# Half-width level products and selects in the recurrent stage of a two-block transformer kernel

## What is computed

```
b = jnp.cumsum(lf, axis=2)
o_inter = jnp.einsum('bhtk,bhkv->bhtv', q * jnp.exp(b), state)
diff = b[:, :, :, None, :] - b[:, :, None, :, :]
decay = jnp.exp(jnp.where(causal[:, :, None], diff, NEG_BIG))
scores = jnp.einsum('bhtk,bhsk,bhtsk->bhts', q, k, decay)
o_intra = jnp.einsum('bhts,bhsv->bhtv', scores, v)
```

## Time and profile before

| | |
|---|---|
| median of 3 runs | 1531.72 us |
| lowest and highest run | 1528.85 and 1534.35 us |
| span of the profiled execution | 1527.0 us |
| PE busy | 1477.4 us, 97% of the span, 7613 instructions |
| DVE busy | 811.7 us, 53% |
| ACT busy | 573.6 us, 38% |
| POOL busy | 317.6 us, 21% |
| the stage of this case | from 1043.2 to 1096.8 us of the span |
| TensorE clock, mean of the span | 0.996 of full speed |

### The profile page before, as it was taken

How to read it: one execution, slowest core, us unless ns; L and a number is a source line. 1 busy time by engine, 2 the same in 40 slices (tenths; PEclk the granted TensorE clock), 3 DMA queues, 4 the chain that set the end, 5 groups by cost and what they waited for, 6 DMA issues and landing times. The chain is left out here.

```text
span 1527.0 us, 18721 instructions
## 1 busy us (share of the span) xinstructions
PE 1477.4 (97%) x7613; PEld 1203.3 (79%) x7613; DVE 811.7 (53%) x1122; ACT 573.6 (38%) x905; POOL 317.6 (21%) x304
## 2 busy tenths in 40 slices
PE   7999999999999999999999999999899999999998
PEld 5888787886788888888887776676778888888886
DVE  4232434578656537433355699878846434333425
ACT  4231534457635413223144532385434323112312
POOL 1000100000023897000002289634421000000000
PEclk9999999999999999999999999999999999999999
DMA  4231222220032323232332222110013323232322
GB/s 186 84 110 61 81 67 94 77 84 1 29 128 79 111 83 111 83 110 83 110 110 66 92 75 84 62 56 29 29 56 111 110 83 111 83 110 83 110 70 82
DMA packets 38858, 129.25 MB, mean 85 GB/s; under 512 B 4676, under 2 KB 23004, under 8 KB 27380
## 3 DMA queue, kind: packets, MB, share of 16 engines
q1 hardware_dynamic: 38484, 127.93, 24.4%
q10 hardware_dynamic: 288, 0.12, 0.0%
HBM read 124.82 MB, written 3.17 MB: 84 GB/s over the span
## 5 line engine op out<-in xcount | busy, mean ns | idle before, releaser
L266 PE MATMUL bank<-xT_hi,ring_hi 128*128 128x512 f32 (+2 forms) x928 | 355.2, 383 | 7.2 <-DVE xT_lo L1728 4.8
L266 PE MATMUL bank<-xT_hi,ring_lo 128*128 128x512 f32 (+2 forms) x928 | 351.7, 379 | 0.0
L266 PE MATMUL bank<-xT_lo,ring_hi 128*128 128x512 f32 (+2 forms) x928 | 351.6, 379 | 0.0
L247 DVE TENSOR_TENSOR ring_lo<-ring_raw,ring_hi 128x2048 fp32r<-128x2048 f32 (+3 forms) x112 | 260.2, 2325 | 168.8 <-ACT ring_hi L233 168.6
L233 ACT CAST ring_hi<-ring_raw 128x2048 fp32r<-128x2048 f32 (+4 forms) x114 | 211.0, 1852 | 240.6 <-DMA ring_raw<-in_w_ff 130.6
L266 PEld LDWEIGHTS bank<-xT_hi,ring_hi 128*128 128x128 f32 (+1 forms) x928 | 174.1, 188 | 47.9 <-issue 7.8
L266 PEld LDWEIGHTS bank<-xT_hi,ring_lo 128*128 128x128 f32 (+1 forms) x928 | 174.0, 187 | 33.9
L266 PEld LDWEIGHTS bank<-xT_lo,ring_hi 128*128 128x128 f32 (+1 forms) x928 | 174.1, 188 | 32.6
L266 PE MATMUL bank<-ring_hi,hid_hi 128*128 128x512 f32 x416 | 162.0, 390 | 0.0
L266 PE MATMUL bank<-ring_hi,hid_lo 128*128 128x512 f32 x416 | 161.9, 389 | 0.0
L266 PE MATMUL bank<-ring_lo,hid_hi 128*128 128x512 f32 x416 | 161.9, 389 | 0.0
(11 more groups left out here) (505 smaller groups left out, 2155.8 us busy)
## 6 DMA issues: line engine op xcount, KB each, us to landing
ring_raw<-in_w_ff SPq DMA_DIRECT2D x30, 1024.0 KB, 4.8
ring_raw<-in_w_up SPq DMA_DIRECT2D x22, 1024.0 KB, 4.8
ring_raw<-in_w_proj SPq DMA_DIRECT2D x8, 1024.0 KB, 5.1
ring_raw<-in_w_gates SPq DMA_DIRECT2D x8, 1024.0 KB, 4.9
ring_raw<-in_w_fm SPq DMA_DIRECT2D x12, 512.0 KB, 5.0
ring_raw<-in_w_dn_a SPq DMA_DIRECT2D x6, 1024.0 KB, 4.8
ring_raw<-in_w_proj SPq DMA_DIRECT2D x8, 512.0 KB, 4.5
ring_raw<-in_w_out SPq DMA_DIRECT2D x4, 1024.0 KB, 4.8
```

The costliest lines, as they stand in the source:

```text
L247: k.nc.vector.tensor_tensor(k.ring.lo[:, g % SLOTS, 0:n], k.raw[:, g % SLOTS, 0:n], plain(k.ring.hi[:, g % SLOTS, 0:n]), ALU.subtract).the ...
L266: mm = k.nc.tensor.matmul(out, x, y, start=first and n == 0, stop=last and n == 3 * len(pairs) - 1)
```

## The change

Levels 1 to 7 use only the right-half columns. The moving operand of a product becomes the 64 tokens of a tile that lie in right halves (a strided pattern over Z), its result is written densely, 64 columns a tile, so that a head's bank is filled to column 256. The predicated copy then reads 256 dense columns, and reads the mask and writes `acc` in a strided pattern of runs of n elements. The columns that are left out are those where the mask was zero. Level 0 keeps its form (`if i == 0`), levels 8 and 9 as well. Nothing is added, removed or reordered: the number of instructions on every engine stays.

```
                 elif n <= 64:
-                    mask = k.mask_lev[:, i, :].bitcast(mybir.dt.uint16).unsqueeze(1).to_broadcast([P, T, P])
-                    x = v.copy_predicated(rows(acc[:, h, :]), mask, rows(ps[:, :]))
+                    m = P // (2 * n)
+                    mask = k.mask_lev[:, i, :].bitcast(mybir.dt.uint16).rearrange("p (b c h) -> p b c h", c=2, h=n)[:, :, 1, :]
+                    dst = acc[:, h, :].rearrange("p (t b c h) -> p t b c h", t=T, c=2, h=n)[:, :, :, 1, :]
+                    x = v.copy_predicated(dst, mask.unsqueeze(1).to_broadcast([P, T, m, n]),
+                                          ps[:, 0:S // 2].rearrange("p (t b h) -> p t b h", t=T, h=n))
...
-                if n <= 64:
+                if i == 0:
                     blocks = [(t * P, t * P, P, t * P) for t in range(T)]
+                elif n <= 64:
+                    blocks = [(t * P, t * P, P // 2, t * P // 2) for t in range(T)]
...
-                            mm = nc.tensor.matmul(k.pb[2 * f + odd][:, c:c + w], L[:, s0:s0 + P], R[:, t0:t0 + w],
-                                                  start=True, stop=True, skip_group_check=True)
+                            out, moving = k.pb[2 * f + odd][:, c:c + w], R[:, t0:t0 + w]
+                            if 1 <= i and n <= 64:
+
+                                moving = R[:, t0:t0 + P].rearrange("p (b c h) -> p b c h", c=2, h=n)[:, :, 1, :]
+                                out = out.rearrange("p (b h) -> p b h", h=n)
+                            mm = nc.tensor.matmul(out, L[:, s0:s0 + P], moving, start=True, stop=True,
+                                                  skip_group_check=True)
```

## The result

The changed kernel takes **1548.82 us** (median of 4 runs, 1543.76 to 1556.74) beside 1530.74 us for the kernel before in the same session: a ratio of **1.0116, interval 1.0091 to 1.0141**. It is 18 us slower; the forecast was 1529.9 us, and its range ended at 1533.4. The profiled execution of after took 1543.76 us, 1542.0 of them its span: 15.0 us more than the span of before. The four runs of the changed kernel lie in two pairs, 1543.76 and 1544.28 us with a mean clock of 0.983 and 0.985, and 1553.36 and 1556.74 us with 0.974 and 0.972. Only the fastest has a profile, so what follows explains 15 us; the other pair took 9 to 13 us more at a lower mean clock, and where they lost it is not recorded.

A forecast was written before the change was run, and what follows sets the result against it. DVE was taken to bound the early levels, PE the work behind decay 8 and the stage. A stage gain of 3.5 us less a clock fall of 1.7 gave -1.8 from 1531.72: 1529.9 us, range 1525.6 to 1533.4.

The forecast's parts named there:

- The clock: Levels 1 to 7 and the wait before decay 8: one fall to 1.2 GHz behind that wait, costing 1.7 us.
- the place at 176 us: Between 176 and 182 us the clock fell after short 64-row products and a 0.69 us wait; 1.7 us of PE's work lost.
- the sum: Whole program: stage gain of 3.5 us less a clock fall of 1.7 us, net -1.8 us, giving 1529.9 us.
- The clock falls again and again: Rival, levels 2 to 7: falls at 1.7 us each, three give 1533.3 us, five 1536.7; chance 0.10.
- The copies: DVE's predicated copies: four of a level fall from 2.56 to 1.48 us, 7.6 us of DVE's time over seven levels.
- the lower end: DVE's copies: no gain if short runs, single elements at level 1, cost as much as the columns saved.
- Up to the exponential of level 5: Levels 2 and 3: PE wins only its waits there, 1.06 us, so ACT's exponential comes 1.1 us earlier.
- The products: no gain on PE: PE's products in levels 1 to 7: weight loads set the pace, so half the moving columns gain nothing.
- Level 6, the collision with L3260: DVE's L3275 of level 8 stands behind POOL's L3260, takes about 2.6 us, and ends only 1.1 us early.
- Level 7 and POOL's power: Level 9 on DVE: POOL's power does not block L3275 and L3276; L3276 takes 0.7 us, Z ready 3.9 us earlier.
- The end: Level 9 starts 3.2 us earlier, the 0.24 us wait before `mix` 3 goes; stage ends 3.5 us earlier.
- what is late next: Before level 5's exponential: once DVE runs 1.08 us ahead per level, PE is late next; DVE's second microsecond is lost.

The follow-up runs named there:

- experiment 2: Changed kernel with half products written to their old places in the bank and the whole 512-column copies of before: 1555.67 us, ratio 1.0136 to before.
- experiment 3: Two versions of the changed kernel: 14 fill products in PE's wait before decay 8, 1551.09 us; 4 fills ahead of each of levels 1 to 7, 1549.69 us.
- experiment 5: Changed kernel, products of levels 1 to 7 reading a tile's first 64 tokens without stride instead of the right halves: 1547.46 us, ratio 1.0102 to before.
- experiment 7: Version of experiment 1 with its masks stored densely in 64 of 128 columns: 1533.17 us in its one run.
- experiment 6: Version of experiment 1 with the products of levels 1 to 3 over 64 moving columns, levels 4 to 7 whole: 1536.83 us, ratio 1.0036 to before.
- experiment 1: Changed kernel with whole products again (128 moving columns), predicated copies still half: 1531.83 us, ratio 1.0013 to before.
- experiment 8: Before with half copies at levels 3 to 7, whole products, two POOL instructions moved, fills in two PE waits: 1528.75 us, ratio 0.9977; also run without fills or POOL moves.

## Why the prediction was wrong

**The step that failed is "The clock".** It saw that the change makes seven levels like the place at 176 us, and that the wait before decay 8 would grow to 1.4 us (it was 1.53), with a fall behind it. In the profile all of that came, one fall, where it was expected. The place was partly luck: with the same half products the fall came at level 1 or 2 in the profiles of experiments 2, 3 and 5, and the slower runs of the changed kernel have no profile. But its price was taken as a constant: "what was lost there is ... 1.7 us". That is the price where the following products bring the clock back. Measured behind decay 8: 37.4 us at 1.2 GHz and a net loss of 13.15 us, where the sum had a gain of 2.4 and a fall of 1.7, a net gain of 0.7. With whole products the constant holds at this very place: 3.69 us for level 5 in experiment 7, 1.63 more than the 2.06 at full clock. A fall was priced by its length at one place, and nobody asked what would end it. The same hole is in the rival "The clock falls again and again": it counted falls at 1.7 us each and needed three, and the case that came, one fall that doesn't end, was in no list. The range of 1525.6 to 1533.4 left out all of it, and 0.05 for a time above 1536.3 was far too little. By the rival's own price four falls make 1535.0, so that only five or more lie above 1536.3.

What the prediction knew of this was that weight loads pace PE at full clock; the profile after shows it at 1.2 GHz too. In the stretch from 1070 to 1106 us the groups by form have

```profile
L3403 PEld LDWEIGHTS bank<-hg_z 64*128 64x128 f32 x128 | 14.8, 327 | 1.7 <-issue 0.8
```

against 187 ns in the earlier trace rows. A level takes 3.68 us at 1.2 GHz with 64 columns and 3.66 with 128 (experiments 6 and 1). PE "busy" for 37.18 of 37.40 us therefore says nothing of how many columns it streams, and this is what the half products halve. That it is this which keeps the clock down is shown for the products as a whole, by experiments 1, 2, 6 and 7; in what measure it counts is open (experiment 3). The Trainium skill, "TensorE: Matmul & The Clock Gate", Part 1, ties the clock to how busy PE has been, 1.2 GHz when idle and 2.4 GHz once busy. With "busy" as the profile counts it, the clock would have come back soon after decay 8, and the time would have been within the range, like the 1531.83 us of experiment 1. The measurement decides otherwise: with PE busy 75.00 of 75.00 us in experiment 3 it didn't.

**The copies.** Forecast 1.48 us for four at every level; measured 1.42 to 1.44 from level 3 on and 2.43 to 2.45 at levels 1 and 2 in experiment 1, where PE holds no copy up. There the lower end, "short runs cost DVE as much as the columns saved", was the right one. The choice had rested on L3276, a plain instruction with single elements two apart; it doesn't carry over to the predicated copy. Of 7.6 us of DVE's time 2 x 0.11 + 5 x 1.14 = 5.9 us were saved.

**Up to the exponential of level 5.** Forecast -1.1 us; measured -0.33 from the stage's start (61.80 - 43.66 against 61.67 - 43.20, times less 1000). As the copies of levels 1 and 2 stayed slow, PE kept its waits: 0.32 us before level 2, 0.23 before level 3, beside 0.30 and 0.26 before.

**The products: no gain on PE.** Right: 2.00 us against 2.06.

**Level 6, the collision with L3260.** Right in experiment 1: 2.48 us, forecast about 2.6. In after it isn't seen: at 1.2 GHz DVE comes when POOL is already in its power.

**Level 7 and POOL's power.** Right: L3275 of level 9 took 0.68 us at 1088.22, inside L3506's 1086.13 to 1089.36, and L3276 behind it 0.68 as well. In after L3275 and L3276 of level 8 took 0.69 and 0.68 us at 1089.44 and 1090.04, inside the power from 1089.06 to 1091.98. The Trainium skill's exclusive lock ("SBUF — State Buffer", "SBUF: two separate sides") agrees with the 2.48 and 2.17 us beside L3260 and L3512 and disagrees with these rows.

**The end.** Forecast 3.2 us before level 9, 2.1 of them behind decay 8, and the wait of 0.24 us before `mix` 3 to go. In experiment 1 the stretch from decay 8 to level 9 takes 19.47 us (1071.53 to 1091.00) against 21.62 before: 2.15 less, as forecast. But the wait grew to 1.48 us: the earlier `finish` ran into POOL's L3512. It was the question "what is late next", not asked of the one POOL instruction that the prediction left out. The prediction counted two collisions; a third stood in the trace of before, on DVE and on POOL:

```profile
1091.71 0.61 DVE L3314 TENSOR_TENSOR ml_den<-ml_den,mcol 128x4 f32<-128x4 f32 x1
```

```profile
1089.50 2.79 POOL L3508 TENSOR_TENSOR hg_silu<-hg_silu,hg_g 128x1024 f32<-128x1024 f32 x1
```

The same instruction takes 0.17 us elsewhere. When DVE comes earlier, it stands behind more of L3508. In experiment 8, with the collisions with L3260 and L3508 moved away and the clock held, the stage gains 3.07 us against the forecast 3.5, but the agreement is partly luck: nothing of it comes before decay 8, where 1.1 was forecast, and behind decay 8, where 2.4 was forecast, the order of POOL is another.

## What to carry to other kernels

Fewer columns per product on PE were no gain here, where weight loads set the pace, and they were a loss: with them the clock did not come back after a short wait. Before pricing a fall of the clock, ask what will end it: look at the products that follow, not at the length of a fall elsewhere. Narrow the side that is the bound (here DVE's copies, from runs of 4 on) and leave the other side's instructions whole, and follow every engine that moves earlier up to the next instruction that it can collide with.

## What the runs showed of the hardware

- The clock of one and the same stretch has two courses. From the same fall at 1050.4 us it is back after 3.4 us with whole products (experiment 1), after 23.8 with three half levels (experiment 6), after 75 with seven half levels and four fills each (experiment 3). From the fall behind decay 8 it is back after 3.4 us with whole products (experiment 7) and after 37.4 with half ones.
- It falls behind waits of PE as short as 0.82 us, but not behind each: the 0.82 us before level 1 was passed at full clock in the profile of before, the 1.49 us before decay 8 in experiment 1, and 1.53 us was not in the changed kernel. The fall of the version with 14 fills began at 1053.0, 2.4 us after its wait of 0.82 us had ended.
- A predicated copy of 256 columns costs 0.61 us (2.45 / 4) in runs of 1 or 2, and 0.36 (1.42 / 4) in runs of 4 and 8; in experiment 1, with runs up to 64, four take 1.42 to 1.44 us.
- A DVE instruction on 128x4, 0.17 us alone (0.17 at 1070.38 in after), takes 2.17 us when it starts 0.20 us behind a POOL instruction on 128x1024 (experiment 1).
